# Turning the residual for the cross-attention queries: from TensorE transposes to VectorE block transposes and transfers

## What is computed

```python
h = rmsnorm(x, norm_mix_w)
mixed = concat(gla(h), diff_attention(h))       # both token mixers, width 512 each
x = x + mixed @ w_out                           # the residual; 7 products "X"
hc = rmsnorm(x, norm_cross_w)
mem_n = rmsnorm(mem, norm_mem_w)                # 256 memory tokens
q = hc @ w_cq                                   # "Q": needs x with features on the partitions
k, v = split(mem_n @ w_ckv)                     # "K", "V"
x = x + softmax(q k^T / 16) v @ w_co            # "SC", "soft", "O", 7 products "Y"
return rmsnorm(x, final_norm_w)
```

## Time and profile before

| | |
|---|---|
| time, median of 3 runs | 818.94 us (818.73 to 819.52) |
| the profiled execution, its own time | 819.04 us |
| its span, first to last instruction | 817.3 us |
| mean granted TensorE clock | 0.998 |
| busy PE, DVE, ACT, POOL | 98%, 72%, 52%, 12% |

### The profile page before, as it was taken

How to read it: one execution, slowest core, us unless ns; L and a number is a source line. 1 busy time by engine, 2 the same in 40 slices (tenths; PEclk the granted TensorE clock), 3 DMA queues, 4 the chain that set the end, 5 groups by cost and what they waited for, 6 DMA issues and landing times.

```text
span 817.3 us, 13056 instructions
## 1 busy us (share of the span) xinstructions
PE 802.3 (98%) x4408; PEld 671.6 (82%) x4408; DVE 589.4 (72%) x1378; ACT 422.1 (52%) x1025; POOL 98.3 (12%) x138
## 2 busy tenths in 40 slices
PE   7999999999999999999999899999999999999996
PEld 6887888888788888888888797888888888888885
DVE  6688677675678678767878877798746454367997
ACT  7766445443455445535445565543745453366443
POOL 3100111121011110111211211010100000001201
PEclk9999999999999999999999999999999999999999
DMA  8321236567455344455677377953422111206945
GB/s 293 116 83 39 85 97 174 94 115 148 77 100 112 84 118 120 83 88 97 129 136 160 89 212 235 315 130 109 156 78 78 38 65 61 69 14 148 216 87 207
DMA packets 105482, 99.22 MB, mean 121 GB/s; under 512 B 41668, under 2 KB 75592, under 8 KB 105416
## 3 DMA queue, kind: packets, MB, share of 16 engines
q1 hardware_dynamic: 81288, 64.30, 26.3%
q0 software_dynamic: 15392, 29.36, 20.1%
q10 hardware_dynamic: 8736, 4.72, 1.9%
HBM read 83.68 MB, written 31.46 MB: 141 GB/s over the span
## 4 chain that ended last, share of the span: by engine, by line
PE 81%; DVE 9%; ACT 3%; DMA 3%; issue 2%; SPq 0%; POOL 0%; ACTq 0%; DVEq 0%
PE bank L1888 14%; PE bank L1890 14%; PE bank L1889 13%; PE banks2to L1888 9%; PE banks2to L1890 9%; PE banks2to L1889 9%; PE banks6to L1951 3%; PE banks2to L2145 3%; DVE w_lo L1408 2%; PE bank L2168 2%; DMA w_raw<-in_w_ckv 2%; DVE neg_max L1690 1%; PE banks2to L2085 1%; PE bank L2170 1%; DVE actT_lo L1407 1%
## 5 line engine op out<-in xcount | busy, mean ns | idle before, releaser
L1890 PE MATMUL bank<-w_hi,actT_lo 128*128 128x512 f32 x412 | 161.4, 392 | 0.0
L1888 PE MATMUL bank<-w_hi,actT_hi 128*128 128x512 f32 x384 | 154.5, 402 | 0.5 <-DVE memT_lo L1407 0.2
L1889 PE MATMUL bank<-w_lo,actT_hi 128*128 128x512 f32 x384 | 149.7, 390 | 0.0
L1408 DVE SCALAR_TENSOR_TENSOR w_lo<-w_raw,vecs,w_hi 128x512 fp32r<-128x512 f32 x120 | 87.2, 749 | 24.5 <-ACT w_hi L1132 24.3
L1890 PEld LDWEIGHTS bank<-w_hi,actT_lo 128*128 128x128 f32 x412 | 77.3, 188 | 16.9
L1132 ACT ACTIVATE w_hi<-w_raw,vecs 128x512 fp32r<-128x512 f32 x120 | 82.8, 719 | 15.1 <-DMA w_raw<-in_w_ckv 9.7
L1888 PEld LDWEIGHTS bank<-w_hi,actT_hi 128*128 128x128 f32 x384 | 72.1, 188 | 16.8 <-DVE w_lo L1408 1.6
L1889 PEld LDWEIGHTS bank<-w_lo,actT_hi 128*128 128x128 f32 x384 | 72.3, 188 | 13.0
L1004 POOL TENSOR_TENSOR rs_o<-var_o,neg_half 128x1 f32<-128x1 f32 (+1 forms) x48 | 31.1, 647 | 344.6 <-DVE var_o L1718 229.4
L1890 PE MATMUL banks2to<-w_hi,actT_lo 128*128 128x512 f32 x164 | 64.0, 390 | 0.0
L1291 ACT ACTIVATE prob<-banks2to,neg_maxs 128x128 f32<-128x128 f32 (+7 forms) x64 | 46.9, 740 | 15.2 <-DVE neg_maxs L1691 15.1
(11 more groups left out here) (376 smaller groups left out, 2037.8 us busy)
## 6 DMA issues: line engine op xcount, KB each, us to landing
w_raw<-in_w_in SPq DMA_DIRECT2D x56, 256.0 KB, 3.0
out_sums<-in_w_out POOLq DMA_DIRECT2D x11, 1024.0 KB, 9.1
late_sums<-in_w_co POOLq DMA_DIRECT2D x11, 1024.0 KB, 9.0
w_raw<-in_w_ckv SPq DMA_DIRECT2D x32, 256.0 KB, 3.8
w_raw<-in_w_cq SPq DMA_DIRECT2D x32, 256.0 KB, 2.7
stage_in<-in_x SPq DMA_DIRECT2D x8, 512.0 KB, 4.5
mixT<-mixed ACTq DMA_DIRECT2D x16, 256.0 KB, 3.4
x_res<-in_x SPq DMA_DIRECT2D x8, 512.0 KB, 5.9
```

The costliest lines, as they stand in the source:

```text
L1408: return dve.scalar_tensor_tensor(dst, src, scale, hi.bitcast(F32), ALU.mult, ALU.subtract)
L1888: pe.matmul(dst, l_hi, r_hi, start=start, stop=False)
L1889: pe.matmul(dst, l_hi, r_lo, start=False, stop=False)
L1890: return pe.matmul(dst, l_lo, r_hi, start=False, stop=stop)
```

## The change

The turn of the residual goes the way of the mixers' outputs. `hturn` t: VectorE transposes the 32x32 blocks of a whole row tile of `x_res` (two buffers for t < 4, `tile_a` and `tile_b`, each free once the store of t - 2 has landed), SyncE stores it in four bands. `hback` t: ScalarE's queue waits for the store and loads the turned tile to `mixT_sum`. `HS`: ScalarE and VectorE split it from there. Nothing of it is left on TensorE. Stages HT are gone, the squares are reordered, `loadw` (the final norm's weights) stands three stages later, and the loads of row tiles 4 and 5 of x move two steps up, behind K(5) and K(6), where they follow the loads of w79 and w80.

```diff
-        if n in (3, 4):
-            plan.append(("loadx", n + 1))
+        if n in (1, 2):
+            plan.append(("loadx", n + 3))
...
-                plan.extend([("xa", 5, t), *([("xa", 6, t)] if t < 2 else [("xr", t - 2)])])
+                plan.extend([("xa", 5, t), *([("xa", 6, t)] if t < 2 else [("xr", t - 2), ("hturn", t - 2)])])
             elif p == 5:
-                plan.extend([("xr", t + 2)] if t < 2 else [])
+                plan.extend([("xr", t + 2), ("hturn", t + 2)] if t < 2 else [("hback", t - 2)])
...
-            if (p == 5 and t > 1) or (p == 6 and t < 2):
-                plan.extend([("HT", (t - 2) % 4, kk) for kk in range(2)])
+            if p == 6:
+                plan.extend([("hback", 2)] if t == 0 else [])
+                plan.extend([("HS", 2 * (t - 1) + j, kk) for j in range(2) for kk in range(2)] if 0 < t < 3 else [])
             if p == 5 and t > 1:
                 plan.append(("xa", 6, t))
             if p == 6:
-                plan.extend([("nsq", 2 * t), ("nsq", 2 * t + 1)] if t < 2 else [])
-                plan.extend([("nsq", TT // 2 + t), *([("loadw",)] if t == 0 else [])])
+                plan.extend([("nsq", n) for n in ((0, 1), (2,), (3, 4), (5, 6, 7))[t]])
+                plan.extend([("hback", 3)] if t == 0 else [])
+                plan.extend([("loadw",)] if t == 3 else [])
...
-        plan.extend([split(u + 1, 0), head("soft", u), query(u + 1, 1), split(u + 1, 1)])
+        plan.extend([split(u + 1, 0), head("soft", u), *([("hback", 4), *turned_rest(6)] if u == 0 else [])])
+        plan.extend([query(u + 1, 1), split(u + 1, 1), *([("hback", 5), *turned_rest(7)] if u == 0 else [])])
+        plan.extend([("hback", 6), ("hback", 7)] if u == 1 else [])
...
+    def turned_rest(t):
+        return [("hturn", t)]
+
+    plan.extend([query(0, 0), split(0, 0), *turned_rest(4), query(0, 1), split(0, 1), *turned_rest(5)])
...
-    plan.extend([("Qa", *query(last, 1)[1:]), ("HT", 4, 0), ("HT", 5, 0), query(last, 1), split(last, 1), ("HT", 6, 0)])
-    plan.extend([older[0], ("HT", 7, 0), older[1], *turned(last - 1), head("SC", last)])
-    plan.extend([("HT", 4, 1), newer[0], ("HT", 5, 1), newer[1], ("HT", 6, 1), ("HT", 7, 1), ("Qa", *query(XH, 0)[1:])])
+    plan.extend([("Qa", *query(last, 1)[1:]), *[("HS", t, 0) for t in range(4, TT)], query(last, 1), split(last, 1)])
+    plan.extend([("HS", 4, 1), ("HS", 5, 1), older[0], ("HS", 6, 1), older[1], ("HS", 7, 1), *turned(last - 1)])
+    plan.extend([head("SC", last), *newer, ("Qa", *query(XH, 0)[1:])])
...
+                elif kind == "hturn":
+                    t = w[0]
+                    sp.wait_ge(md_dve, DIFF_STEPS + t + 1)
+                    for first, n, tile in turning_tile(t):
+                        for band in range(P // BLK):
+                            part = tile[BLK * band:BLK * band + BLK, :]
+                            sp.dma_start(turned_rows(first, n, t, band),
+                                         part.rearrange("r (b c) -> r b c", c=BLK)).then_inc(d_mixd[t % 4], 16)
...
+                elif kind == "hback":
+                    t = w[0]
+                    act.wait_ge(*turned_stored(t))
+                    if t < 4:
+                        act.wait_ge(*matmuls_done(("X", 4, t)))
+                    act.dma_start(mixT_sum[:, :, cols(t)],
+                                  mixed[:, cols(t)].rearrange("(k p) c -> p k c", p=P)).then_inc(d_tile[t % 4], 16)
+                elif kind == "HS":
+                    t, kk = w
+                    act.wait_ge(*residual_back(t))
+                    if t < 4:
+                        sum_ready(act, ("asum", "s4", t // 2))
+                    else:
+                        act.wait_ge(w_used, W0[GROUP_OF[("Q", 0, XH - 1, 1)]] + KT // 2 * (1 + kk))
+                    raw, hi, _ = kept_residual(t, kk)
+                    copy(hi, raw).then_inc(xa_act, 1)
...
+                elif kind == "hturn":
+                    t = w[0]
+                    if t >= 4:
+                        dve.wait_ge(*matmuls_done(("X", 6, 3)))
+                    dve.wait_ge(*row_ready(t))
+                    if t % 4 >= 2:
+                        dve.wait_ge(*turned_stored(t - 2))
+                    for first, n, tile in turning_tile(t):
+                        last = dve.transpose(tile, x_res[:, t, first:first + n])
+                    last.then_inc(md_dve, 1)
+                elif kind == "HS":
+                    raw, hi, lo = kept_residual(*w)
+                    dve.wait_ge(*residual_back(w[0]))
+                    dve.wait_ge(xa_act, SPLIT_X[stage] + 1)
+                    lo_part(lo, raw, hi).then_inc(xa_dve, 1)
...
-                elif kind == "HT":
-                    t, kk = w
-                    pe.wait_ge(*row_ready(t))
-                    turn(stage, [x_res[:, t, cols(4 * kk + j)] for j in range(4)])
                 elif kind in ("Qa", "Q"):
...
-                    pe.wait_ge(ring_dve, TR[("HT", 4 * half + 3, 0 if kind == "Qa" and h + d == 0 else 1)] + 1)
+                    kk = 0 if kind == "Qa" and h + d == 0 else 1
+                    pe.wait_ge(xa_dve, SPLIT_X[("HS", 4 * half + 3, kk)] + 1)
```

More of the change, by code:

```diff
@@ L274, in attend @@
         plan.extend([query(u + 1, 0), head("SC", u)] + (turned(u - 1) if u % XH else []))
-        plan.extend([split(u + 1, 0), head("soft", u), query(u + 1, 1), split(u + 1, 1)])
+        plan.extend([split(u + 1, 0), head("soft", u), *([("hback", 4), *turned_rest(6)] if u == 0 else [])])
+        plan.extend([query(u + 1, 1), split(u + 1, 1), *([("hback", 5), *turned_rest(7)] if u == 0 else [])])
+        plan.extend([("hback", 6), ("hback", 7)] if u == 1 else [])
         plan.extend([("ya", 0, 0), ("ya", 0, 1)] if u == 2 * XH - 2 else [])
         plan.extend(mixed_values(u - 1) if u % XH else [])
-    plan.extend([query(0, 0), split(0, 0), query(0, 1), split(0, 1)])
+    def turned_rest(t):
+        return [("hturn", t)]
+    plan.extend([query(0, 0), split(0, 0), *turned_rest(4), query(0, 1), split(0, 1), *turned_rest(5)])
     for u in range(XH - 2):
@@ L429 @@
 TQK_BANK = [1, 7] + [7 if i % TT < 4 else 1 for i in range(DIFF_STEPS - 2)]
-TR = rings({"T", "HT", "PT"})
-SPLIT_X = rings({"xa"})
+TR = rings({"T", "PT"})
+SPLIT_X = rings({"xa", "HS"})
 SUMMED = {stage: n for n, stage in enumerate(
@@ L725, in build @@
         ring_raw = sem("mixed_tiles_kept")
-        mg_dve, md_dve = sem("gla_mix_turned"), sem("diff_mix_turned")
+        mg_dve, md_dve = sem("gla_mix_turned"), sem("diff_mix_and_residual_turned")
         sum_dve = sem("weight_sums")
@@ L862, in ring_job, with turning_tile, turned_stored, residual_back @@
                 return cpT_hi[:, w[2], :], cpT_lo[:, w[2], :], ps
-            t, kk = w
-            c = cols(t % 4)
-            return (actT_hi[:, 4 * kk:4 * kk + 4, c], actT_lo[:, 4 * kk:4 * kk + 4, c],
-                    ps.rearrange("p (j c) -> p j c", j=4))
+        def turning_tile(t):
+            if t < 4:
+                return [(0, D, (tile_a, tile_b)[t % 2][:, :])]
+            return [(WC * j, WC, mixT[:, 6 - 2 * (t % 2) + j, 4 * P:8 * P]) for j in range(2)]
+        def turned_stored(t):
+            return d_mixd[t % 4], STORED * (DIFF_STEPS // 4 + (1 if t < 4 else 3))
+        def residual_back(t):
+            return d_tile[t % 4], 16 * (len(RELOADS) // 4 + t // 4 + 1)
+        def kept_residual(t, kk):
+            rows, c = slice(4 * kk, 4 * kk + 4), cols(t % 4)
+            return mixT_sum[:, rows, cols(t)], actT_hi[:, rows, c], actT_lo[:, rows, c]
         def query_keys(i):
@@ L980, in _ @@
                 elif kind == "loadw":
+                    sp.wait_ge(*turned_stored(3))
                     sp.dma_start(tile_b[:, :], a["final_norm_w"].partition_broadcast(P)).then_inc(d_fw, 16)
@@ L1261, in _ @@
                     copy(hi, src).then_inc(xa_act, 1)
-                elif kind in ("T", "HT", "PT"):
+                elif kind in ("T", "PT"):
                     act.wait_ge(ring_pe, TR[stage] + 1)
```

## The result

The changed kernel takes 830.04 us (median of 4 runs, 829.18 to 832.17) where the kernel before took 818.84 on the same chip (818.43 to 819.52): a ratio of 1.0144 with a 95% interval of 1.0123 to 1.0165, so 11.2 us slower. 824.2 was forecast, in a range of 819 to 830. The sign and the chain of events came as told; the size is twice the 5.3 us forecast. The profiled execution took 829.18 us with a span of 827.4, 10.1 above the span before.

The account below looks back on a forecast made before the run. TensorE, 98% busy, was taken to bound the kernel. 819.04 - 3.5 (second half's transposes) - 1.3 (loads of x) + 8.4 (later Q(0, 0)) + 1.7 (clock) = 824.3, or 824.2 as a median, range 819 to 830.

Parts of the forecast that it names:

- What bounds the kernel: TensorE, busy 98%: each instruction removed is worth its time if operands are ready; 64 transposes at 0.109 us, 7.0 us.
- What moves: Two loads of x moved up: w87's load lands sooner, winning back 1.3 of 1.6 us lost in the second value group.
- Step 1: VectorE's four transposes, 1.24 us each: w115 split at 580.6 or later, X(6, 0) waits 1.3 us or more, hidden.
- Step 2: The stores: 4096 packets take the engines 3.1 us, an issue 0.43; a lone store lands 4.6 us after its first issue.
- (c): Rival, slower still: issues with 1024 packets cost 1.68 us each, 5 us more per tile on SyncE; 829.3 us; chance 0.08.
- Step 3: Turned tiles 2 and 3 wait for stores to free their buffers: VectorE stands still up to 1.6 us.
- Step 4: w119's load behind the stores on SyncE's queue: issues done near 582, w119 lands between 583.8 and 590.
- Step 5: ScalarE's list behind w119, 12.1 us: Q(0, 0) between 595.9 and 602.1, taken at 600.0, 8.4 us later than before.
- Step 6: TensorE's clock falls after some 9 us idle ahead of Q(0, 0): 1.7 us added, bounds 0 and 3.4.
- (a): Rival: transfers do not queue, Q(0, 0) at 595.9, 820.2 us, no change a measurement can tell; chance 0.14.
- (b): Rival, faster: the turn is hidden, w119 split by 581.5, ScalarE's list ends at 592.9, 815.5 us; chance 0.12.
- (d): Rival: the loads of x hold back V(1, 0), 1.5 us lost instead of 1.3 gained, 827.0 us; chance 0.05.

Follow-up runs that it names:

- second_half: Changed kernel with tokens 0 to 511 turned by TensorE as before, only 512 to 1023 by the new route: 816.01 us against 819.19, again 816.35 against 819.38.
- loads_alone: Kernel before with only the two loads of x moved up, behind K(5) and K(6): 818.39 us against 819.19, ratio 0.9993.
- second_old_loads: second_half with all loads of x where the kernel before has them: 815.40 us against 819.61, ratio 0.9955.
- no_turning: Changed kernel without VectorE's transposes of tokens 0 to 511; the stores read x_res itself, with no wait for a free tile: 829.89 us, ratio 1.013.
- quarter_store: Changed kernel with three of the four bands of each store of tokens 0 to 511 cut to 32 columns: 824.69 us, ratio 1.0074.
- store_behind_weights: two_more_early with row tile 1's store issued behind w119's load and its load back behind ScalarE's first squares: 820.41 us against 818.92, ratio 1.0019.
- filler_long: Changed kernel with 96 unused identity transposes on TensorE ahead of Q(0, 0): 829.13 us, ratio 1.0124.
- one_more_early: second_half plus row tile 0 by the new route, its splits ahead of ScalarE's squares, behind X(6, 0): 815.96 us against 819.38, ratio 0.9964.
- filler: Changed kernel with 70 unused identity transposes on TensorE ahead of Q(0, 0): 831.71 us, ratio 1.0156.
- long_runs: Changed kernel storing the same bytes of tokens 0 to 511 in 512-byte runs, a quarter of the packets: 827.13 us, ratio 1.0106.
- two_more_early: second_half plus row tiles 0 and 1 by the new route, splits behind X(6, 0) and X(6, 1), ahead of the squares: 819.71 us against 819.38, ratio 1.0002.

## Why the prediction was wrong in size

**What bounds the kernel: right.** Work taken off TensorE is worth its time where the rest follows: second_half, -3.0 to -4.2 us for 32 transposes, -3.5 forecast.

**What moves: wrong.** The 1.3 us were read from one execution. loads_alone shows -0.8 us with an interval that holds zero, and second_old_loads loses nothing without the move. X(0, 0) starts anywhere from 510.1 to 513.0 with the loads moved; the 1.6 us of loss at V(1, 0) come and go between executions.

**Step 1: right.** 1.24 us a transpose, w115 at 580.99 (580.6 or later was said), on a clock that runs 1.7 early here, so 2 us behind the earliest said. TensorE waited 4.0 us for it, and that was hidden in the larger wait: in no_turning it is gone and Q(0, 0) comes only 1.1 earlier.

**Step 2: the term that was mis-sized.** Four issues were put at 1.8 us by the 0.43 median of small stores; they took 2.67 to 4.79, 0.92 each in the mean. The bounds, 0.30 and 1.68, held the mean, but the sum used only the median, and rival (c) only the upper end. What an issue costs here is not told by its own packets: the first issue of the first store, 1024 packets, took 0.33; in quarter_store the issues of 32 packets behind the first one took 0.42 to 0.66; and w119's load took 2.36 behind the fourth store, where the weight loads of the kernel before take 0.33 each in this stretch. It grows with what stands ahead of it on its queue: 0.33, 0.57, 0.68 and 0.97 in the first store. The packets themselves cost the engines nearly what was said: from 568.0 to 573.5, 5128 of them took 76.7% of 16 engines, 13.2 ns each against 12.0. The Trainium skill, page "Perfetto Trace Analysis" (DMA Instruction — HWDGE), says that the time shown for an issue runs until all its descriptors have been generated. By the means the trace agrees, 0.92 against 0.65 for the same bytes in a quarter of the packets; but a first issue of 1024 packets in 0.33 and a weight load in 2.36 show that their number alone doesn't set it.

**Step 3: short by 1.2.** The waits for tiles were 0.82 and 2.02 us, 2.8 together where up to 1.6 was forecast: the first store landed 5.6 us after its first issue, not 4.8.

**Step 4: here the error lands.** "SyncE is through store 3's issues: near 582" came out as 585.6, on the old clock 587.3. Its own late end was 582.5 (store 1 landed at 579.5, 1.2 for the transpose, 1.8 for the issues); the other 4.8 are 1.5 for the last transpose, which ended at 582.2 on that clock, 1.3 for the loads of w117 and w118 that SyncE still had to issue, and 2.0 for the four issues. From there w119 took 5.4 us to ScalarE, less than the 8 the forecast's late end allowed, so the load did wait in turn, but less was left ahead of it by then than was counted. On the old clock w119 came at 592.7 instead of 590 at the latest. The count of the engines' work was short too: 18.1 us before w119's own load, where the engines were busy for 22.1 (0.96 of 23.0) from the first store to w119's arrival. The term counts three weight loads where w119's makes four, and puts them at 0.7 apiece. So both the issuing queue, with 14.7 us of store issues between 568 and 585.6, and the engines were full, each longer than forecast. Which of the two holds the other up no run shows, and no bound of step 4 held either. Weights behind stores: store_behind_weights shows it as an effect of order. The Trainium skill's page "DMA: Bandwidth & Descriptors" (Queues, rings and completion order), which the forecast leaned on against this change, is borne out in so far; whether the ring on the engines or the issues ahead of it hold the load back, no run separates.

**Step 5: right in length, wrong in the choice.** 12.0 us measured, 12.1 forecast. Q(0, 0) was taken at 600.0 between 595.9 and 602.1; on the old clock it came at 604.7, 2.6 past the late end. Taking less than the late end for "some slack" had no row behind it, and lost 2.1 of the 4.7.

**Step 6: right.** 1.9 measured, 1.7 forecast; filler_long shows that it comes of TensorE standing still.

**The sum.** Against the forecast's 5.3, Q(0, 0) is 4.7 later, the clock 0.2 dearer and the loads, in this one trace, 0.4 better: 9.8 of the 10.1 of the profiled execution; the other 0.3 is what follows Q(0, 0), 3.2 shorter instead of 3.5. The median is 11.2 slower; that the 1.1 more are the early X(0, 0) of the profiled execution, the fastest of the four, fits but isn't shown. Of the rivals, (a) is too low even for quarter_store, 6.2 us above before where (a) had 1.2; (b) is what one_more_early makes of one tile; (c) named the right term and with 829.3 came nearest to the 830.0, but by luck in part: it put an issue at 1.68 where 0.92 was measured, and counted only those of the last store; (d) didn't happen. Remaining open: why issues get slower on a busy queue (0.67 in the mean of the first store, 1.20 in that of the third), since packets and load on the engines changed together in the runs that cut them.

## What to carry to other kernels

Ahead of moving a turn from a busy engine to stores and loads, cost the queue that issues them by what stands ahead of each issue, not by the median of small ones on a quiet queue; add up what the DMA engines then have to move, weight loads included; and ask which weight load stands behind the last store. The same route was hidden where tens of us lay between turn and use, and cost some 14 us (11.2 + 3.2) where 18 to 24 did, from `xr` 3 and `xr` 0 to Q(0, 0): the version to keep is the one that turns only the second half this way, 815.4 to 816.4 against 819.2 to 819.6. When one engine works in a fixed order, the place of the new operations in that order (ahead of squares that nobody waits for soon) can be worth as much as the operations, 6.3 us here. The Trainium skill's page "VectorE: DVE Perf Modes" (Rules for kernel authors) says to transpose 128×128 on TensorE if the result may be in PSUM; the first half bears it out, the second half is faster against it.

## What was not expected of the hardware

The granted clock fell behind waits of TensorE of 2.7 us (filler), 2.9 us (store_behind_weights) and 4.0 us, all from full work right before, and the matmuls behind ran at 0.43 us spacing instead of 0.23, eight of them in the changed kernel and in store_behind_weights. It did not fall behind the 1.1 us of store_behind_weights, nor behind the 2.2 of no_turning, nor behind a wait of 2.9 in long_runs, ahead of 581.52:
```profile
582.00:584.00 2.00, 2.00 (x11) 1.62 (x10) 2.00 (x5) 1.86 (x3) 0.00 (x0) 1.00 0.90 214
```
So a wait of 3 us costs 3 or nearly 5, and its length alone doesn't tell which; behind the 4.0 of two_more_early the clock took 2.4 more. In the changed kernel the fall behind the 4.0 us wait at 581.72 is free, since the next wait swallows it.
